# Output projections of a two-branch mixer as three products of upper and lower parts, in place of plain 32 bit

## What is computed

```
y_a = nsa_attention(...) @ w_proj_nsa          # (256 x 512) @ (512 x 1024)
y_b = gla_attention(...) @ w_proj_gla          # (256 x 512) @ (512 x 1024)
mixed = jax.nn.sigmoid(m_a) * y_a + jax.nn.sigmoid(m_b) * y_b
return mixed @ w_out                           # (256 x 1024) @ (1024 x 1024)
```

## Time and profile before

| | |
|---|---|
| median of 3 runs | 1291.72 us (1288.10 to 1292.69) |
| the profiled execution's own time | 1292.28 us |
| its span in the trace | 1290.5 us |
| TensorE busy | 1191.1 us, 92% |
| VectorE, ScalarE, GpSimd busy | 464.1, 421.1, 221.1 us |
| mean granted TensorE clock | 0.978 of full |
| stage of the change, start to end | from 242.1 us (transposes) to 317.7 us (end of `out1`) |

### The profile page before, as it was taken

How to read it: one execution, slowest core, us unless ns; L and a number is a source line. 1 busy time by engine, 2 the same in 40 slices (tenths; PEclk the granted TensorE clock), 3 DMA queues, 4 the chain that set the end, 5 groups by cost and what they waited for, 6 DMA issues and landing times.

```text
span 1290.5 us, 17989 instructions
## 1 busy us (share of the span) xinstructions
PE 1191.1 (92%) x6932; PEld 737.0 (57%) x6932; DVE 464.1 (36%) x1031; ACT 421.1 (33%) x806; POOL 221.1 (17%) x327
## 2 busy tenths in 40 slices
PE   7998988899999999998989999998999899999996
PEld 6786655557523234324344324425897687899775
DVE  3567245443400002123223012115366545444554
ACT  4554243333310001032323000203434463444772
POOL 3005365100000000001111000002431222201450
PEclk9999899799999999999999999999999999999999
DMA  9656398243589999999999999996742113665300
GB/s 363 208 176 254 100 328 315 98 149 116 197 341 409 409 409 408 392 403 408 409 405 408 406 408 407 394 409 231 228 131 97 53 33 114 187 189 183 113 18 33
DMA packets 97035, 333.63 MB, mean 259 GB/s; under 512 B 10416, under 2 KB 10672, under 8 KB 96816
## 3 DMA queue, kind: packets, MB, share of 16 engines
q1 hardware_dynamic: 96944, 332.41, 69.1%
HBM read 331.32 MB, written 1.05 MB: 258 GB/s over the span
## 4 chain that ended last, share of the span: by engine, by line
PE 67%; DMA 17%; DVE 5%; ACT 4%; issue 2%; POOL 2%; SPq 1%; DVEq 0%; POOLq 0%; ACTq 0%
PE ps L455 24%; DMA w<-in_w_gate 7%; DMA w<-in_w_up 6%; PE ps L2342 6%; PE ps L1794 5%; PE ps L507 4%; PE ps L787 3%; PE ps L2394 3%; DMA w<-in_w_down 3%; PE ps L799 3%; PE ps L816 2%; PE ps L1356 2%; PE ps L929 2%; PE ps L1813 2%; PE ps L2370 1%
## 5 line engine op out<-in xcount | busy, mean ns | idle before, releaser
L2342 PE MATMUL ps<-w,vT 128*32 128x512 f32 x1024 | 193.3, 601 | 14.5 <-DMA w<-in_w_gate 7.8
L439 ACT ACTIVATE ab<-w 128x1024 fp32r<-128x1024 f32 (+2 forms) x117 | 121.9, 1048 | 181.0 <-PE ps L455 168.3
L449 DVE TENSOR_TENSOR ab<-w,ab 128x1024 fp32r<-128x1024 f32 (+2 forms) x96 | 118.1, 1237 | 156.0 <-ACT ab L439 156.0
L2342 PEld LDWEIGHTS ps<-w,vT 128*32 128x32 f32 x1024 | 38.0, 108 | 149.8 <-issue 63.5
L455 PE MATMUL ps<-ab,uA 128*128 128x512 f32 x320 | 104.2, 408 | 4.7 <-DVE uB L1395 2.2
L1794 PE MATMUL ps<-w,Uc 128*128 128x512 f32 (+1 forms) x224 | 99.7, 591 | 0.0
L455 PE MATMUL ps<-UA,ab 128*128 128x256 f32 x512 | 92.8, 283 | 0.4 <-POOL UB L572 0.4
L455 PE MATMUL ps<-ab,UA 128*128 128x512 f32 (+1 forms) x288 | 87.8, 386 | 0.4 <-POOL UB L572 0.4
L2394 PE MATMUL ps<-w,bT 128*32 128x512 f32 x512 | 78.5, 598 | 9.8 <-ACT bT L2447 5.5
L455 PEld LDWEIGHTS ps<-UA,ab 128*128 128x128 f32 x512 | 80.1, 192 | 1.3 <-POOL UB L572 1.2
L455 PEld LDWEIGHTS ps<-ab,uA 128*128 128x128 f32 x320 | 61.4, 194 | 20.5 <-issue 4.2
(11 more groups left out here) (521 smaller groups left out, 1884.0 us busy)
## 6 DMA issues: line engine op xcount, KB each, us to landing
w<-in_w_gate SPq DMA_DIRECT2D x128, 512.0 KB, 10.8
w<-in_w_up SPq DMA_DIRECT2D x128, 512.0 KB, 11.7
w<-in_w_down SPq DMA_DIRECT2D x128, 512.0 KB, 11.8
w<-in_w_ada SPq DMA_DIRECT2D x48, 512.0 KB, 7.5
w<-in_w_c SPq DMA_DIRECT2D x48, 512.0 KB, 4.4
w<-in_w_m SPq DMA_DIRECT2D x16, 512.0 KB, 5.1
w<-in_ab_out_w SPq DMA_DIRECT2D x16, 512.0 KB, 8.1
w<-in_w_out SPq DMA_DIRECT2D x8, 512.0 KB, 5.4
```

Source lines behind the costliest of these rows:

```text
L439: e.activation(sp.a(j), w.v, ACT.Copy).then_inc(sp.whole, 1)
L449: e.tensor_tensor(sp.b(j), w.v, sp.a(j).bitcast(F32), ALU.subtract).then_inc(sp.parts[j % NAB], 1)
L2342: ins = e.matmul(t.ps[o, :], ve[:, p % 2, 2 * c + k, o], w.v[:, k, :], start=c + k == 0, stop=c + k == 4)
```

## The change

The four plain products become split ones. The branches' rows are split into `yA`, `yB`, `oA`, `oB` (ScalarE the upper part, VectorE the lower); their weights go through the list `S1` between the chunks of `m01`, `m11` and `out0`; `pe_lin_steps` gets a number of chunks `n` (2 here); the calls of `act_splits` and `rest_splits` are placed anew. The arrays lie over others that are dead by then.

```diff
-        def pe_lin_steps(e, sp, name, A, B, cols, tiles, on_pool=(), ring_=None):
+        def pe_lin_steps(e, sp, name, A, B, cols, tiles, on_pool=(), ring_=None, n=4):
...
-                for n, x, p in (("ynT", ynT, "pnsa"), ("ogT", ogT, "pgla")):
+                for n, A, B, p in (("ynT", yA, yB, "pnsa"), ("ogT", oA, oB, "pgla")):
                     if c == 1 and n == "ogT":
                         pe_context_norm(e)
-                    for i in range(2):
-                        ts, t = slice(i * 128, (i + 1) * 128), bank.take(ALL, p + str(c))
-                        free(e, t)
...
-                        for k in range(4):
-                            w = W[f"{p}{c}.{k // 2}"]
...
-                            ins = e.matmul(t.ps[:, :], x[:, k, ts], w.v[:, k % 2, :], start=k == 0, stop=k == 3)
...
+                    if c == 0:
+                        all_emptied(e, n)
+                    for _ in pe_lin_steps(e, S1, p + str(c), A, B, 512, range(2), n=2):
+                        pass
...
-            t = bank["ynT"][0]
-            e.wait_ge(t.full, t.n)
-            e.activation(ynT[:, :, 0:128], blocks(t), ACT.Copy).then_inc(t.evac, 1)
+            act_splits(e, S1, "pgla0.0")
+            for i, t in enumerate(bank["ynT"]):
+                e.wait_ge(t.full, t.n)
+                e.activation(yA[:, :, i * 128:(i + 1) * 128], blocks(t), ACT.Copy).then_inc(upper_out, 1)
+            for i, t in enumerate(bank["ogT"]):
+                e.wait_ge(t.full, t.n)
+                for k in range(4):
+                    ins = e.activation(oA[:, k, i * 128:(i + 1) * 128], blocks(t)[:, k, :], ACT.Copy, scale=S("glang")[:, k:k + 1])
+                ins.then_inc(upper_out, 1)
+            act_splits(e, S1, "pgla0.1")
             for i in range(2):
                 e.activation(grow[:, i, :], grow[:, i, :], ACT.Sigmoid).then_inc(gates, 1)
+            act_splits(e, S1, "m11.1")
             for i in range(2):
                 e.activation(xsm[:, i, 0, :], xsm[:, i, 0, :], ACT.Sigmoid).then_inc(gates, 1)
             act_lin(e, S1, "m11", [xsm[:, i, 1, :] for i in range(2)], ACT.Sigmoid, scaled=True)
+            act_splits(e, S1, "pgla1.1")
...
-                    e.tensor_copy(ynT[:, :, i * 128:(i + 1) * 128], blocks(t)).then_inc(t.evac, 1)
...
-                e.tensor_tensor(ogT[:, :, i * 128:(i + 1) * 128], blocks(t), bc(S("glang"), 2, 128), ALU.mult).then_inc(t.evac, 1)
-            rest_splits(e, "dve", S1, "m11.2")
+            rest_splits(e, "dve", S1, "pgla0.0")
+            for i, t in enumerate(bank["ynT"]):
+                o = (slice(None), slice(None), slice(i * 128, (i + 1) * 128))
+                e.wait_ge(upper_out, n_upper.up())
+                e.tensor_tensor(yB[o], blocks(t), yA[o].bitcast(F32), ALU.subtract).then_inc(t.evac, 1)
+            for i, t in enumerate(bank["ogT"]):
+                e.wait_ge(upper_out, n_upper.up())
+                for k in range(4):
...
+                    ins = e.scalar_tensor_tensor(out=oB[o], in0=blocks(t)[:, k, :], scalar=S("glang")[:, k:k + 1], in1=oA[o].bitcast(F32),
+                                                 op0=ALU.mult, op1=ALU.subtract)
+                ins.then_inc(t.evac, 1)
+            rest_splits(e, "dve", S1, "m11.0")
             for c in range(2):
...
                 for i in range(2):
+                    rest_splits(e, "dve", S1, f"m11.{1 + i}" if c == 0 else "pgla1.1")
```

More of the change, by code:

```diff
@@ L250, in build @@
         gr = m("gr", [128, 2, 512])
+        ends = [m.at]
         la, cum, tmp = (m(n, [128, 2, 256]) for n in ("la", "cum", "tmp"))
+        ends.append(m.at)
         Am = m("Am", [128, 4, 3, 128])
+        ends.append(m.at)
         qT = m("qT", [128, 4, 256])
+        ends.append(m.at)
         kT = m("kT", [128, 2, 4, 256])
@@ L256, in build @@
         ones = K[:, 0, :]
+        yB, oB, yA, oA = (Region(at, TOP)(n, [128, 4, 256], F32R) for n, at in zip(("yB", "oB", "yA", "oA"), ends))
         m = Region(12 * SLOT, TOP)
@@ L338, in build @@
         vcd = xs[0:120, 0, 0:512]
-        ynT, ogT = qT, kT[:, 0]
         grown = bP[:, 0:2, :].rearrange("p a n -> p (a n)")
@@ L456, in three @@
             return ins
-        def pe_lin_steps(e, sp, name, A, B, cols, tiles, on_pool=(), ring_=None):
+        def pe_lin_steps(e, sp, name, A, B, cols, tiles, on_pool=(), ring_=None, n=4):
             use_ = {i: bank.take(ring_ or ALL, name) for i in tiles}
-            for c in range(4):
+            for c in range(n):
                 j = sp.add(f"{name}.{c}", c in on_pool)
@@ L470, in pe_lin_steps @@
                         x = 2 * c + k
-                        ins = three(e, t.ps[:, 0:cols], (A[:, x, ts], B[:, x, ts]), (a[:, k, 0:cols], b[:, k, 0:cols]), x == 0, x == 7)
-                    if c == 3:
+                        ins = three(e, t.ps[:, 0:cols], (A[:, x, ts], B[:, x, ts]), (a[:, k, 0:cols], b[:, k, 0:cols]), x == 0, x == 2 * n - 1)
+                    if c == n - 1:
                         ins.then_inc(t.full, 1)
-                if c < 3:
+                if c < n - 1:
                     sp.gone(j, ins)
@@ L1342, in pe_first @@
                     pe_lin(e, S1, "m11", uA, uB, 512, range(2))
-                for n, x, p in (("ynT", ynT, "pnsa"), ("ogT", ogT, "pgla")):
+                for n, A, B, p in (("ynT", yA, yB, "pnsa"), ("ogT", oA, oB, "pgla")):
                     if c == 1 and n == "ogT":
                         pe_context_norm(e)
-                    for i in range(2):
-                        ts, t = slice(i * 128, (i + 1) * 128), bank.take(ALL, p + str(c))
-                        free(e, t)
-                        if i == 0 and c == 0:
-                            e.wait_ge(*emptied(n, 0))
-                            e.wait_ge(*emptied(n, 1))
-                        for k in range(4):
-                            w = W[f"{p}{c}.{k // 2}"]
-                            if i == 0 and k % 2 == 0:
-                                e.wait_ge(w.full, w.n)
-                            ins = e.matmul(t.ps[:, :], x[:, k, ts], w.v[:, k % 2, :], start=k == 0, stop=k == 3)
-                        ins.then_inc(t.full, 1)
-                    for k in range(2):
-                        W.release(f"{p}{c}.{k}", t.full, t.n)
+                    if c == 0:
+                        all_emptied(e, n)
+                    for _ in pe_lin_steps(e, S1, p + str(c), A, B, 512, range(2), n=2):
+                        pass
             e.wait_ge(mix_done, 4)
@@ L1662, in dve_first @@
             beside(dve_attend(e, NSA, V_), rest)
[L1663 to L1666, removed]
-                    e.tensor_copy(ynT[:, :, i * 128:(i + 1) * 128], blocks(t)).then_inc(t.evac, 1)
-                t = bank["ogT"][i]
-                e.wait_ge(t.full, t.n)
-                e.tensor_tensor(ogT[:, :, i * 128:(i + 1) * 128], blocks(t), bc(S("glang"), 2, 128), ALU.mult).then_inc(t.evac, 1)
-            rest_splits(e, "dve", S1, "m11.2")
+            rest_splits(e, "dve", S1, "pgla0.0")
[6 more added lines that the diff above has]
+                for k in range(4):
+                    o = (slice(None), k, slice(i * 128, (i + 1) * 128))
+                    ins = e.scalar_tensor_tensor(out=oB[o], in0=blocks(t)[:, k, :], scalar=S("glang")[:, k:k + 1], in1=oA[o].bitcast(F32),
+                                                 op0=ALU.mult, op1=ALU.subtract)
+                ins.then_inc(t.evac, 1)
+            rest_splits(e, "dve", S1, "m11.0")
             for c in range(2):
```

## The result

The changed kernel takes 1294.36 us in the median of 20 runs (1290.70 to 1298.60), the kernel before 1290.67 us beside it (20 runs, 1285.39 to 1292.73): ratio 1.0035, 95% interval 1.0024 to 1.0046, about 4.5 us. (The ratio is taken over all the runs; the two medians alone differ by 3.7 us.) The profiled execution took 1294.25 us with a span of 1292.4.

The account below looks back on a forecast made before the run. TensorE, or what it waits for, was taken to set the time up to the experts. Terms -0.1 + 1.15 + 0.8 + 1.2 - 0.9 gave +2.2 us on 1292.28, then 0.56 off for the median: 1293.9 us, range 1288.0 to 1298.0.

Parts of the forecast that it names:

- Products: Four plain products become split: each falls from 6.87 to 5.46 us, saving 5.6 us of TensorE in all.
- Start: First split product waits for weight subtractions and yn's lower parts: TensorE starts at 246.9 instead of 245.92, +1.0 us.
- The ring of three: Weight chunks are ready before TensorE needs them; the tightest, m11.0, is covered by 1.4 us.
- The middle: Before the context transposes, ScalarE's squares wait behind a weight copy: TensorE idles 3.2 us, 4.0 us of gain become 0.85.
- Tile 0 after three quarters: In pgla1 tile 0 fills after three quarters, 4.1 us plus 0.2; VectorE's 6 us tail starts where it did.
- `out0`: First chunk no longer split ahead, so TensorE starts out0 at 295.2 instead of 294.03: +1.15 us.
- The clock: Half-clock terms: +0.8 us at the start, +1.2 around the context transposes and pgla1, -0.9 at out0.
- The price of a stretch at half clock: Half clock after a wait costs 1.9 us: out's eight chunks took 23.68 us, against 21.8 at 0.227 per matmul.
- The passing gain: Rival: context rows are not late, so TensorE's saving passes on: -3.5 us, 1288.2 us; chance 0.11.
- absorbed by the experts' stage: Rival: the experts' DMA stream starts from slots freed earlier, so the 2.2 us vanish: 1291.7 us; chance 0.15.
- the clock rival: Rival: clock falls at the start, before the context transposes and before out0: +8.25 us, 1300.0 us; chance 0.08.
- little to do: Observation on the kernel before: clock is half up to 247 us and at 295, each after TensorE had little work.

Follow-up runs that it names:

- e_rows: Changed kernel with the context's squares and two scaled rows moved earlier, into ScalarE's idle time: ratio to before 1.0009.
- e_tile: Changed kernel with pgla1 computed token tile by token tile, so tile 0 is whole after half the product: ratio to before 1.0028.
- b_more0: Kernel before, plain products kept, with the first three chunks of out0 no longer split ahead of mxT: ratio to before 1.0011.
- b_free: Kernel before, plain products kept, with yn's transposes ahead of go's and the context's squares and scaled rows early: ratio to before 0.9978.
- e_start: Changed kernel with yn's transposes ahead of go's and two weight subtractions instead of three ahead of yn's lower parts: ratio to before 1.0018.
- e_out0: Changed kernel with out0.0 to out0.2 copied ahead of mxT's upper parts and out0.0 subtracted ahead of its lower parts: ratio to before 1.0015.
- a_fill: Changed kernel with 20 thrown-away products on TensorE in its 4.6 us wait ahead of the mxT transposes: ratio to before 1.0024.
- e_all: Changed kernel with context rows early, out0 chunks split ahead, pgla1 tile by tile and the start reordered: ratio to before 0.9933, repeated 0.9944.

## Why the prediction was right

The median lies in the range and 0.5 us over the number named, and the sign and the class were right. The nearness is luck in part: the forecast was +2.2 us, and the change cost 4.4 in the stage and 4.5 in the ratio. The base was too high by 1 us, since before's median over 20 runs is 1290.67, not the 1291.72 of the three I had. The steps, one by one, changed kernel against before:

- *Products.* Forecast -1.41 us each, with `m11`'s 0.227 us for a matmul. In the new products one takes 0.234 at full clock (18 in 4.21 us, 12 in 2.81), so a product takes 5.60 us and saves 1.27, 5.1 us for the four in place of 5.6. The order was as described. Right but for this size; why these run slower than `m11`'s is open. By the estimate in the prediction, from the pages "TensorE: Matmul & The Clock Gate" (section "Wait — 56ns, not 53.3ns?") and "FP8 and Floating Point Precision" (section "TensorE Precision Notes") of the Trainium skill, it would have been 6.9. The trace lies on the other side of the rows: 0.234 us, and 0.230 in `out` (22.05 us for 96), not 0.216.
- *Start*, forecast +1.0: 247.76 - 243.11 = 4.65 against 3.82, +0.8. Right; the `og` rows were covered, as said.
- *The ring of three*, forecast no wait inside: 120 matmuls in one piece. Right.
- *The middle*, forecast an idle of 3.2 us, behind which 0.85 of the gain remains at full clock: 2.91, ended by ScalarE's row, and 0.85 (A-B is 1.15 longer than before, 2.0 of that by the clock at the start). `e_rows` shows that it was this. Right.
- *Tile 0 after three quarters*: 4.21 us in place of 3.45; forecast 4.3. `e_tile` shows it. VectorE's tail 5.95 us, unchanged. Right.
- *`out0`*, forecast +1.15 for the lost lead: `b_more0` says 1.0. Right.
- *The clock*, forecast 0.8 (start) + 1.2 (middle) - 0.9 (`out`) = +1.1. Measured 2.0 (start: 29.72 less 27.7, which is 72 matmuls at 0.2335 and `m11`'s 10.9 us), 0 (middle), 1.4 (in the `mxT` transposes) and 0 (`out`): +3.4. **This is the step that failed**, in size and in place, in this execution and its repeat. The start lies just over its bounds of 0 to 1.9, and the lower one was a slip: the sum runs the new products at full clock throughout, so a rise of the clock as early as before would still have cost the 0.8 that before paid. The fall that I put at the context transposes did not come, and one that I had not thought of came at `mxT`, after TensorE's idle of 4.6 us behind `pgla1`. That idle was 2.55 us before; the quicker product (1.3) and the later tile 0 (0.8) made it longer. In the prediction's terms the stage is -0.1 + 1.0 + 3.4 = 4.3 us, not 2.2. Laid out by stretches against before: 3.8 saved by three products, against 0.8 at the start, 1.2 more of clock behind it than the 0.8 of before, 2.9 idle (A-B, +1.1); 0.8 for the later tile 0 (B-C); 1.0 for the lead and 1.4 of clock (C-D). The fourth product's saving is nowhere on the path. The price of a stretch at half clock, 1.9 us in the prediction, was too high as well: `out` takes 22.05 us at full clock, not 21.8, so it is 1.6.

The passing gain did not happen, for the reason given. Nothing was absorbed by the experts' stage, as far as the profiles tell: behind the stage both executions of the changed kernel took 969.3 us and the plain products of `b_free` 969.7; the 972.8 of before went with four stretches at half clock. Of the three gaps of the clock rival the start cost its ceiling (2.0 against 1.9 us), the middle one nothing, and the last 1.4 in the transposes ahead of `out0`. The Trainium skill's page "TensorE: Matmul & The Clock Gate", section "HAM oscillation — how this bites in real kernels", tells of a kernel that starts each burst of matmuls at half clock after waits of 3 to 5 us. The trace agrees for the last gap (4.6 us idle, 16 transposes in 3.61 us). The middle one, 2.91 us, is just short of the page's waits, and the clock stayed at 1.00 behind it; but in `e_start` the same idle ended with transposes at 3.12 us.

## What to carry to other kernels

A faster product is worth what the next wait leaves of it: ahead of such a change, follow each wait behind the products to its releaser and ask how long before its use it is ready. Here 2.9 us, out of 3.8 that three products had saved, were lost to one row, which now ended 0.1 us before its use; moved into idle time of the same engine, it gave them back. New splits pushed into an in-order engine's list delay what stands behind them: count the leads they take away (`more=3`, 1.0 us here) as a cost of their own. And when a change frees an engine, look at whether a consumer could start on the first half of a product (`pgla1` tile by tile: VectorE began 1.4 us earlier in the trace).

## What was not expected

The runs of one kernel spread over 10 us, and it goes with the clock. Of the 95 timed runs of the kernel before in these series, the 24 with a mean granted clock of 0.983 or more took 1286.9 us in the mean, the 14 with 0.978 or less 1292.4. The mean clock over the changed kernel's 20 runs is 0.9792, over before's 95 runs 0.9810. By the line through the 95 runs that is an estimated 1.7 us: so part of the 4.5 us is the clock, in the timed runs as in the profile. And the same idle of 2.91 us in the same place ended with the clock full in five profiles (the changed kernel twice, `e_out0`, `e_tile`, `a_fill`: transposes in 2.15 us) and with it falling in one (`e_start`, 3.12 us). The same wait of 3.18 us ahead of the `mxT` transposes ended with 2.06 us for them in `e_tile` and 3.64 in `e_all`:

```profile
288.61 2.06 PE L542 MATMUL ps<-cst,grow 128*128 128x128 f32 x16 [3.18 <-DVE grow L1722]
```
```profile
283.15 3.64 PE L542 MATMUL ps<-cst,grow 128*128 128x128 f32 x16 [3.18 <-DVE grow L1729]
```

One could not tell it from the wait's length. Nor does the prediction's "little to do" fit the start: in the kernel before TensorE was busy for 6.5 of the 7 us from 239 to 246 us, with small products and transposes, and the clock read 0.50 throughout.
